# A VectorE step of the first attention: the half steps of the linear attention move ahead of bias and maximum

## What is computed

```python
h = rmsnorm(x, norm1_w)
proj = h @ w_in
aq, ak, av, bq, bk, bv, br, ba, cq, ck, cv = jnp.split(proj, ...)
y_a = dilated_attention(heads(aq, A_HEADS), heads(ak, A_HEADS), heads(av, A_HEADS), bias_a)
y_b = gla(heads(bq, B_HEADS), heads(bk, B_HEADS), heads(bv, B_HEADS), br, ba, w_a2, b_a, gla_norm_w)
y_c = moba_attention(heads(cq, C_HEADS), heads(ck, C_HEADS), heads(cv, C_HEADS), bias_c)
x = x + jnp.concatenate([y_a, y_b, y_c], axis=-1) @ w_out
```

```python
diff = b[..., :, None, :] - b[..., None, :, :]
decay = jnp.exp(jnp.where(causal[:, :, None], diff, NEG_INF))
attn = jnp.einsum('bhnic,bhnjc,bhnijc->bhnij', qc, kc, decay)
o_intra = jnp.einsum('bhnij,bhnjv->bhniv', attn, vc)
```

## Time and profile before

| | us |
|---|---|
| median of 3 runs | 2368.41 (2367.79 to 2371.66) |
| the profiled execution, its own time | 2373.12 |
| its span | 2371.3 |
| TensorE busy (matmuls) | 2281.4, 96% |
| VectorE busy | 1416.5, 60% |
| ScalarE busy | 903.2, 38% |
| GpSimd busy | 513.5, 22% |
| mean granted TensorE clock | 0.984 of full speed |

### The profile page before, as it was taken

One profiled execution on the slowest core, in us unless ns is written; L12 is line 12 of the kernel. 1 busy time (PEld: TensorE's weight loads), 2 busy tenths in 40 slices (PEclk: granted clock), 3 DMA queues, 4 the chain that ended last, 5 costly groups with the idle time before them and its releaser, 6 DMA issues.

```text
span 2371.3 us, 30166 instructions
## 1 busy us (share of the span) xinstructions
PE 2281.4 (96%) x11618; PEld 1886.9 (80%) x11618; DVE 1416.5 (60%) x2332; ACT 903.2 (38%) x1521; POOL 513.5 (22%) x363
## 2 busy tenths in 40 slices
PE   8989799999999998989999999999899999999998
PEld 6655587888887875668999999999676578888887
DVE  4575657889757457763675565544736775434335
ACT  4344533332343325882522222122432794423232
POOL 3332223332322210001312121111121002322221
PEclk9999899999999999999999999999999999999999
DMA  5211017555421331001244343431123002323321
GB/s 182 80 54 54 27 36 264 183 195 195 151 85 53 103 106 44 19 19 36 92 136 128 123 133 124 135 102 58 56 98 101 26 28 80 98 89 101 104 89 54
DMA packets 76250, 227.71 MB, mean 96 GB/s; under 512 B 9151, under 2 KB 12608, under 8 KB 76108
## 3 DMA queue, kind: packets, MB, share of 16 engines
q1 hardware_dynamic: 72368, 217.80, 27.4%
q0 software_dynamic: 1856, 6.07, 0.7%
q10 hardware_dynamic: 1884, 1.91, 0.2%
HBM read 220.99 MB, written 4.76 MB: 95 GB/s over the span
## 4 chain that ended last, share of the span: by engine, by line
PE 86%; DVE 7%; ACT 4%; issue 2%; POOL 1%; DMA 0%; DVEq 0%; ACTq 0%; SPq 0%; POOLq 0%
PE psum L777 32%; PE psum L1100 25%; PE psum L851 3%; PE psum L746 3%; PE psum L1478 3%; PE psum L798 3%; PE psum L1509 2%; PE psum L871 2%; PE psum L1432 2%; PE psum L1360 1%; PE psum L1493 1%; PE psum L1124 1%; PE psum L683 1%; PE psum L1445 1%; PE psum L1319 1%
## 5 line engine op out<-in xcount | busy, mean ns | idle before, releaser
L777 PE MATMUL psum<-mix_split,weight_split 128*128 128x384 f32 (+1 forms) x3072 | 623.4, 363 | 5.1 <-DVE residual L1986 3.0
L777 PEld LDWEIGHTS psum<-mix_split,weight_split 128*128 128x128 f32 x3072 | 557.8, 189 | 67.0 <-issue 3.9
L1100 PE MATMUL psum<-hidden,weight_split 128*128 128x512 f32 (+1 forms) x2880 | 584.5, 363 | 0.0
L1100 PEld LDWEIGHTS psum<-hidden,weight_split 128*128 128x128 f32 x2880 | 521.4, 188 | 59.8
L2506 ACT CAST weight_split<-weight_ring 128x1024 fp32r<-128x1024 f32 x269 | 277.4, 1041 | 288.6 <-PE psum L1100 221.1
L3132 POOL TENSOR_TENSOR weight_split<-weight_ring,weight_split 128x1024 fp32r<-128x1024 f32 x89 | 232.1, 2608 | 503.0 <-ACT weight_split L2506 502.8
L2001 DVE TENSOR_TENSOR hidden<-hidden_tmp,hidden 128x512 fp32r<-128x512 f32 (+1 forms) x98 | 138.5, 1415 | 313.8 <-POOL hidden_tmp L3274 313.8
L3274 POOL TENSOR_TENSOR hidden_tmp<-hidden_tmp 128x512 f32<-128x512 f32 (+1 forms) x98 | 126.2, 1289 | 588.6 <-ACT hidden L2804 588.4
L1582 DVE TENSOR_TENSOR weight_split<-weight_ring,weight_split 128x1024 fp32r<-128x1024 f32 x180 | 227.9, 1267 | 40.5 <-ACT weight_split L2506 40.5
L2798 ACT ACTIVATE hidden_tmp<-psum 128x512 f32<-128x512 f32 (+1 forms) x94 | 62.7, 667 | 465.3 <-PE psum L777 465.0
L2024 DVE SCALAR_TENSOR_TENSOR residual<-psum,modulation,residual 128x512 f32<-128x512 f32 (+3 forms) x232 | 117.7, 551 | 135.3 <-PE psum L1100 135.0
(11 more groups left out here) (349 smaller groups left out, 2917.5 us busy)
## 6 DMA issues: line engine op xcount, KB each, us to landing
weight_ring<-in_w_mlp SPq DMA_DIRECT2D x128, 512.0 KB, 4.0
weight_ring<-in_w_ff SPq DMA_DIRECT2D x64, 512.0 KB, 4.8
mod_ring<-in_w_mod SPq DMA_DIRECT2D x48, 512.0 KB, 3.9
late_ring<-in_w_mod SPq DMA_DIRECT2D x96, 256.0 KB, 3.7
weight_ring<-in_w_in SPq DMA_DIRECT2D x45, 512.0 KB, 3.7
weight_ring<-in_w_out SPq DMA_DIRECT2D x24, 512.0 KB, 3.7
weight_ring<-in_tables SPq DMA_DIRECT2D x13, 512.0 KB, 3.7
weight_ring<-in_w_v SPq DMA_DIRECT2D x8, 512.0 KB, 4.8
```

The costliest lines, as they stand in the source:

```text
L777: m = pe.matmul(psum[:, b + r, 0:hi - lo], w[:, part_w, :], moving(x, part_x, k, lo, hi), start=k == 0 and part_w + part_x == 0, stop=k == ...
L1100: mm = pe.matmul(psum[:, b + r, 0:hi - lo], w[:, part_w, :], G[:, part_x, f % (2 * GROUP), lo:hi], start=jj == 0 and part_w + part_x == 0, ...
```

## The change

In VectorE's `mixers` the two half steps of a step are issued behind `prob_t(n)` and ahead of `exps(n + 4)`, `mix` and `keep`, as long as the counter is below 50; from step 11 on the order is the old one. Nothing else differs, and the other engines' programs are the same.

```diff
@@ -1917,13 +1917,17 @@
                         if n + 3 < len(ATT):
                             inverse_sum(n + 3)
                         prob_t(n)
+                        first = at[0] < PAIR + 2 * B_CHUNK
+                        if first:
+                            half_tick()
+                            half_tick()
                         if n + 4 < len(ATT):
                             exps(n + 4)
                         if n == 4 * u and u and u % 2 == 0:
                             mix(u // 2 - 1)
                         if n == 4 * u + 2 and filler(u) is not None:
                             keep(filler(u))
-                        for _ in range(2):
+                        for _ in range(0 if first else 2):
                             half_tick()
                             if at[0] - 1 in SPLIT_MIX:
                                 split_mix_1(SPLIT_MIX[at[0] - 1])
```

## The result

| | before | after |
|---|---|---|
| median of 7 runs, us | 2368.41 (2366.24 to 2371.98) | 2377.3 (2374.31 to 2381.3) |
| the profiled execution, its own time | 2373.12 | 2377.23 |
| its span | 2371.3 | 2375.4 |

The ratio is 1.0029 with an interval of 1.0017 to 1.0041: slower by 6.9 us (4.0 to 9.7, the ratio times the median before). The medians differ by more, 8.9 us. The forecast was 5.1 us slower, at 2373.5 us; the median came out 3.8 us above that, inside the stated range of 2367 to 2379.5.

A forecast was written before the change was run, and what follows sets the result against it. TensorE was taken as the bound (86% of the span), with VectorE's order counting only where TensorE waits. Step-by-step lateness came to 5.1 us, which put the median of 2368.41 at 2373.5 us, range 2367 to 2379.5.

The forecast's parts named there:

- The mechanism: TensorE's product waits (line 905 for 1763) fall under 2 us; waits for copies, biases and, in steps 1 to 10, exponentials appear.
- Steps 0 to 2: Loop bodies for items 0 to 2: logits 0.4 us earlier, then a late projection copy makes the next projection 1.5 late.
- The clock of step 4's half: Half projection near 131 us, behind some 2.5 us of idleness: slower clock costs 1.5 us (bounds 0 and 1.6), 3.0 late.
- Steps 3 to 6: VectorE paces: logits in step 4 come 4.6 us late (2.8 without the long addition), the projection after step 6 4.8 late.
- the long addition: VectorE addition inside GpSimd's weight subtraction, 2.15 us instead of 0.4; hit again, sum 5.1 us late, without it 3.3.
- The rule of the port lock: A two-SBUF-input VectorE operation and a GpSimd one reading SBUF lock each other out; the first to start keeps the port.
- Steps 7 and 8: VectorE's lateness ends in 5.67 us of idle time; a 1.97 us wait goes, projection 2.0 nearer, logits 14 late by 2.6.
- step 10: The projection's copy is last again and ends only 1.2 us nearer than before: late by 3.6.
- The clock of step 12's half: Half projection near 162 us, behind 2.6 us of idleness: slower clock costs 1.5 us (bounds 0 and 1.6), 5.1 late.
- The rival that ended faster: Bank waits go and nothing replaces them: 7 to 8 us gained, 2361 us; chance 0.10.
- the copy of step 2: ScalarE's copy emptying the projection's bank: must end by 129.6 us for the faster rival; forecast to end at 131.05.

## Why the prediction came out as it did

**The mechanism** held: the product waits fell to 0.5 us by the matmuls (under 2 forecast; 3.5 by the weight loads), and the copies (2.31, 0.95, 2.67) and the biases (2.19, 2.30, 1.19) took their place. The reciprocals waited 0.56 to 0.88 us in steps 2 to 6, 8 and 10, not in each step from 1 to 10: in steps 1, 7 and 9 other work of VectorE lay between. The lateness of the last matmuls of the stretch is that of the end (5.4 and 5.4).

**Steps 0 to 2, sized too small.** 1.5 forecast, 3.1 measured, the term that failed. I let the clock fall only in the half projection of step 4. It fell earlier, behind the idle time ahead of the logits; the stretches of 2 us (us, busy, granted clock, DMA share, GB/s) show it:

```profile
122.00:124.00 2.00, 0.00 (x0) 1.00 0.00 0
124.00:126.00 2.00, 1.96 (x8) 0.72 0.00 0
126.00:128.00 2.00, 1.62 (x7) 0.50 0.00 0
...
166.00:168.00 2.00, 0.53 (x2) 1.00 0.75 110
```

So the products of step 2 ran at the 1.2 GHz level too: the first product took 1.24 us (125.04) against 0.65 before, and VectorE waited 0.82 us for the first. The logits themselves were 0.2 late and not 0.4 early, since the multiplication of step 0 had to wait 0.52 us for its product, which I had taken as ready. With both, the first multiplication of step 2 stands 1.3 us behind the forecast (11.7 us from step 0 against 10.4), and an addition of 0.71 us instead of 0.46 makes the copy 1.5 late against it (16.1 against 14.6).

**The clock of step 4's half** was right (4.71 us, 1.7 more than before, for 1.5 forecast). **Steps 3 to 6** were right in their differences: 3.0 to 4.8 forecast, 4.8 to 6.8 measured, with the long addition at 2.12 us. The terms written out for step 6 add up to 147.5 and not to the 148.1 that the forecast used: from the start of the logits it allowed 0.55 us to the multiplication, and it took 1.1 (144.72 to 145.84), so the larger figure was the better one. The rule of the port lock that I had weighed (the Trainium skill, SBUF — State Buffer, "Who interferes with whom") agrees with the trace in both kernels (2.15 and 2.12 us for the addition beside the subtraction); moving the subtraction away made the addition short, and where the subtraction happened to start behind it (the reciprocal moved), it was short as well.

**Steps 7 and 8** gave back 1.9 us (2.0 forecast), **step 10** took its copy as forecast (0.8 for 1.0).

**The clock of step 12's half, sized too large.** 1.5 forecast, 0 measured: 2.97 us at a clock of 1.00 behind a wait of 2.67 us. This error and that of step 2 had opposite signs, and the sum came out at 5.1 against 5.4 by more luck than the terms deserve. The runs put the loss at 6.9 and the medians at 8.9, so against them the forecast is on the low side.

**The rival that ended faster** did not come, and its deciding point, the copy of step 2, was the right one: with three copies early the loss is gone. What I had not asked is what early copies gain by themselves. The earlier trace rows show 0.6 us for them up to 164 us, and I had not read the 5.0 us behind the stretch, since the change doesn't go there.

What stays open: where the last us of the some 6 comes from that the early copies gain in the later units beyond the 5.0 booked on them, what the other nine steps cost beside early copies, and how much of single runs' differences of 1 to 3 us is the clock, which fell in some executions and not in others at the same place of the same code (below).

## What to carry to other kernels

Before an engine's work is moved forward, list what it passes and who empties what behind it: here the order was good for the waits it went at and bad for a copy of 0.6 us that frees the only bank of the largest consumer. Such a small operation is the first to try ahead of everything else on its engine; here that gained 6.6 us where the reordering lost 6.9. The reordering gained where its engine came in idle, which one row of the timeline tells, so it is worth trying there before it is made over a whole phase. And when an experiment shortens a wait, look whether another event moved with it: the moved reciprocal also took an addition out of the reach of a GpSimd operation.

## What was not expected of the hardware

The granted clock answers to the same code differently from run to run. In 76 executions of the kernel before, beside the experiments, its mean over the kernel ran from 0.983 to 0.989: the fastest, 2364.22 us, had 0.989, and the six above 2375 us had 0.983 to 0.985. Up to the projection of step 2, the kernel before and the run with early copies in it have the same order and the same waits of 0.81 and 0.19 us ahead; it took 4.61 us in one and 3.02 in the other. Waits of 2.65 and 2.73 us ahead of step 12's half left that half at 4.30 and 4.24 us (even steps alone; the reciprocal moved), while 2.67 us ahead of the same half gave 2.97 in the changed kernel and 3.01 with the subtraction moved. The rows of the first two stand above. And behind the wait of 2.19 us ahead of the logits of step 2 the next product took 1.24 us in the changed kernel and 0.68 with the subtraction moved, which up to there is the same program.

So a term for the clock of a single stretch is safer carried as a range between its two prices than set at either.
